# Attention's gate: the sigmoid as ScalarE's exponential, with a sum and a reciprocal on VectorE

## What is computed

```python
def diff_attention(q, k, v, rel_bias, lam, lam_init, subln_w):
    ...
        logits = jnp.einsum('bqhmd,bkhmd->bhmqk', q_blk, k).astype(jnp.float32) * scale + bias
        p = jax.nn.softmax(logits, axis=-1)
        attn = p[:, :, 0] - lam * p[:, :, 1]
        return jnp.einsum('bhqk,bkhd->bqhd', attn.astype(v.dtype), v)
    ...
    o = rmsnorm(o, subln_w) * (1.0 - lam_init)

# in hybrid_layer
    proj = jnp.einsum('bsd,de->bse', h, w_in)      # q, k, v and the gate's input ag among it
    o_a = diff_attention(...)
    o_a = o_a * jax.nn.silu(ag)
```

## Time and profile before

| | |
|---|---|
| runs | 3447.71, 3453.41, 3459.82 us (median 3453.41) |
| profiled execution | 3451.49 us |
| its span, from first to last instruction | 3449.7 us |
| mean granted TensorE clock | 0.981 of full speed |
| TensorE busy | 3276.7 us, 95% |
| VectorE busy | 1852.2 us, 54% |
| ScalarE busy | 1423.0 us, 41% |
| GpSimd busy | 436.3 us, 13% |
| attention, layer 0 | 1957 to 2301 us of the span |
| attention, layer 1 | begins some 750 us later |

### The profile page before, as it was taken

One profiled execution on the slowest core, in us unless ns is written; L12 is line 12 of the kernel. 1 busy time (PEld: TensorE's weight loads), 2 busy tenths in 40 slices (PEclk: granted clock), 3 DMA queues, 4 the chain that ended last, 5 costly groups with the idle time before them and its releaser, 6 DMA issues. The chain is left out here.

```text
span 3449.7 us, 73665 instructions
## 1 busy us (share of the span) xinstructions
PE 3276.7 (95%) x32618; PEld 2033.5 (59%) x32618; DVE 1852.2 (54%) x2557; ACT 1423.0 (41%) x2045; POOL 436.3 (13%) x302
## 2 busy tenths in 40 slices
PE   6999999999899797999999899999999999999999
PEld 3446565644444346999886466657644466657544
DVE  4666767662526524666553566654453366754342
ACT  3554545433655422333333445542322255533321
POOL 3000000020000002334331132300000232200000
PEclk9999999999999998999999999999999999999999
DMA  5111111130355552111112111021021211020211
GB/s 177 37 49 46 39 39 34 43 118 17 98 127 123 123 139 77 68 68 56 58 46 87 55 32 54 7 60 32 17 91 49 68 43 37 1 66 26 65 67 49
DMA packets 308210, 214.84 MB, mean 62 GB/s; under 512 B 125403, under 2 KB 283950, under 8 KB 305326
## 3 DMA queue, kind: packets, MB, share of 16 engines
q1 hardware_dynamic: 307464, 210.18, 20.4%
q10 hardware_dynamic: 458, 0.37, 0.0%
HBM read 172.74 MB, written 41.98 MB: 62 GB/s over the span
## 5 line engine op out<-in xcount | busy, mean ns | idle before, releaser
L142 PE MATMUL psum<-u,w_hi 128*128 128x512 f16 x1856 | 555.5, 381 | 17.3 <-PEq L197 5.4
L142 PE MATMUL psum<-u,w_lo 128*128 128x512 f16 x928 | 353.3, 381 | 0.0
L142 PEld LDWEIGHTS psum<-u,w_hi 128*128 128x128 f16 x1856 | 181.4, 98 | 245.8 <-issue 23.0
L115 DVE SCALAR_TENSOR_TENSOR w_lo<-stage,w_hi 128x1024 f16<-128x1024 f32 x140 | 170.4, 1238 | 217.1 <-ACT w_hi L109 216.5
L174 PE MATMUL psum<-u,w_hi 128*128 128x512 f16 x896 | 271.4, 381 | 0.0
L2650 DVE CUSTOM_DVE_ANT_0 probs_att<-psum,bias_att 128x1024 f32<-128x1024 f32 x128 | 156.8, 1225 | 165.4 <-PE psum L2445 165.0
L1071 PE MATMUL psum<-w_hi,merged 128*128 128x512 f16 x768 | 233.4, 382 | 6.8 <-PEq L3072 4.5
L2423 PE MATMUL psum<-u,w_hi 128*128 128x512 f16 x768 | 232.2, 384 | 6.7 <-PEq L1109 6.7
L1071 PE MATMUL psum<-held_hi_out,merged 128*128 128x512 f16 x768 | 231.2, 379 | 0.0
L97 POOL TENSOR_TENSOR w_hi<-stage,w_scale 128x1024 f16<-128x1024 f32 x36 | 69.1, 1920 | 946.6 <-PE psum L2423 839.3
L190 PE MATMUL psum<-w_hi,u 128*128 128x128 f16 x2048 | 173.2, 219 | 0.0
(11 more groups left out here) (463 smaller groups left out, 6987.6 us busy)
## 6 DMA issues: line engine op xcount, KB each, us to landing
stage<-w_in SPq DMA_DIRECT2D x72, 512.0 KB, 5.0
X<-rwkv_chunks SPq DMA_DIRECT2D x14, 1792.0 KB, 8.1
stage<-ab_w_in SPq DMA_DIRECT2D x48, 512.0 KB, 4.8
stage<-rw_w_in SPq DMA_DIRECT2D x32, 512.0 KB, 4.7
rwkv_chunks<-work_rp SPq DMA_DIRECT2D x26, 512.0 KB, 5.9
stage<-w_out SPq DMA_DIRECT2D x24, 512.0 KB, 4.2
X<-x SPq DMA_DIRECT2D x16, 512.0 KB, 8.5
stage<-ab_w_out SPq DMA_DIRECT2D x16, 512.0 KB, 4.7
```

The lines of the kernel that those rows point to most:

```text
L115: dve.scalar_tensor_tensor(K.w_lo[:, slot, :], K.stage[:, slot, :], W_SCALE, K.w_hi[:, slot, :], ALU.mult, ALU.subtract).then_inc(K.w_full ...
L142: last = pe.matmul(K.psum[:, bank, :], w[:, k, :], u[:, k, cols], start=(k == 0 and n == 0), stop=(k == KT - 1 and n == 2))
```

## The change

ScalarE computes exp(-x) in place of sigmoid(x), and no longer loads the set behind it. VectorE adds 1 and takes the reciprocal, in place on `gate`, and then multiplies as before. Each of the two new instructions is followed by a drain, which lets VectorE finish writing before the next one reads. Nothing else differs; the order of the work is as it was.

```diff
--- before.py
+++ after.py
@@ -2548,10 +2548,8 @@
                     else:
                         if g >= 2:
                             act.wait_ge(part_done, 2 * (g - 1))
-                        act.activation(gate[g % 2][:, cols(half)], bank, ACT.Sigmoid, scale=UNSCALE
+                        act.activation(gate[g % 2][:, cols(half)], bank, ACT.Exp, scale=-UNSCALE
                                        ).then_inc(g_sig, 1)
-                        if g or half:
-                            act.preload_act_table_set("natural_log_exp_and_others")
 
                 def exponentials(s):
                     for m in range(2):
@@ -2637,6 +2635,10 @@
                     elif slot == 3:
                         x = gate[g % 2][:, cols(half)]
                         dve.wait_ge(g_sig, g * 2 + half + 1)
+                        dve.tensor_scalar(x, x, 1.0, None, ALU.add)
+                        dve.drain()
+                        dve.reciprocal(x, x)
+                        dve.drain()
                         dve.scalar_tensor_tensor(x, bank, UNSCALE, x, ALU.mult, ALU.mult).then_inc(taken[half], 1)
 
                 def with_bias(s):
```

## The result

The changed kernel takes 3471.02 us (median of 8 runs, 3462.15 to 3475.42), the kernel before 3448.76 us (median of 8, among them the three shown above). The medians differ by 22 us. The ratio is 1.0059, with a 95% interval of 1.0046 to 1.0073: slower by about 20 us (16 to 25). The forecast was 3467 us, 15.8 us slower.

A forecast was written before the change was run, and what follows sets the result against it. TensorE sets attention's pace, so only late releases count: 9.2 us at heads 1 and 2, 4.8 at head 3, 1.8 at head 0, sum 15.8 us on 3451.49, giving 3467.3 us; range 3457 to 3481.

The forecast's parts named there:

- The table loads at nothing: ScalarE, gates: 28 removed loads of 1.283 us, 35.9 us in all, were costed at no gain.
- The price of a half: VectorE, each of 16 gate halves: sum 0.45, two drains 0.18, reciprocal 3.4, together 4.03 us more.
- The slope of 6.25 ns a column: VectorE's reciprocal: growth from 8 to 12 columns extended to 512, giving 3.35 us; 3.4 us taken.
- Heads 1 and 2: Four gates, both layers: TensorE 2.3 us late at each through late bank releases, 9.2 us in all.
- the first wait: Heads 1 and 2: TensorE waits 0.8 us for the bank released by the first half's product.
- the second wait: Heads 1 and 2: TensorE waits 1.5 us for the second half's release, 2.3 us late in all.
- Head 0: Two gates: first half just in time, bias sums late for TensorE's logits by 0.9 us; 1.8 us in all.
- the rival with GpSimd: Head 0: GpSimd holds the new sum for all three operations, 4.3 us more a layer, 3476 us; chance 0.08.
- Head 3: Last head, two gates: second half's late release delays the next stage 1.9 us in layer 0, 2.9 in layer 1; 4.8 us.
- A reciprocal that is fast at length: VectorE: 512 columns take some 0.7 us, nothing reaches TensorE, 3451.5 us; chance 0.10.
- The loads on the path: ScalarE's table loads delay TensorE, so up to 35.9 us come back, 3431 us at the best; chance 0.04.
- The clock: Heads 1 and 2: granted clock falls behind the new waits, adding 10 to 20 us, 3477 to 3487 us; chance 0.08.

The follow-up runs named there:

- ScalarE's half: Changed kernel without VectorE's sum and reciprocal, exponent scaled down by 1000: exponential for sigmoid, 28 table loads fewer. Ratio to the kernel before 0.9991.
- the last one: Kernel before, sigmoid and table loads kept, with only two order changes at the last head, on ScalarE and VectorE: 3439.28 us, ratio 0.9976.
- the gate of exp, Ln and exp: Changed kernel with ScalarE computing the whole sigmoid as exp, Ln, exp in one table set, no VectorE sum or reciprocal: ratio to before 0.9996.
- the late gate: Changed kernel with the same sums and reciprocals on VectorE behind the bank's release, which ScalarE gives after copying the value: ratio to before 1.004.
- half the columns: Changed kernel with the reciprocal over 256 of each half's 512 columns, exponent scaled down by 1000: ratio to before 1.0021.
- the reciprocal is doubled: Changed kernel with a second reciprocal and drain behind the first, exponent scaled down: ratio to before 1.0256.
- ScalarE's order alone changed: Sigmoid from ScalarE's exp, Ln, exp, with finished values taken ahead of exponentials in steps 24 and 28: ratio to before 0.9986.

## Why the prediction was right

**Point by point.** The table loads at nothing: right, by the experiment on ScalarE's half and by the last one. The price of a half, 4.03 us: right; it is 0.427 + 3.353 + two gaps of 0.08, 3.94 us. The slope of 6.25 ns a column, taken from 4 columns' difference, held up to 512. The reciprocal of 128x512 is not the 4.27 us that eight cycles a column would make of the Trainium skill's repeat count ("VectorE: DVE Perf Modes", "First, the fixed hardware budget"): 6.25 ns are six cycles at its 0.96 GHz.

Heads 1 and 2: 2.3 forecast, 2.48 measured four times. The steps are all there: the first wait (0.8, measured 0.77), the bias sum without its idle time, the small product that swallows the lateness behind GpSimd (1.93 us became 1.11), the second wait (1.5, measured 1.58). The 0.2 us missing come from two small things that I left out: GpSimd's operations, behind which the second half stands, end 0.3 us later (above), against 0.1 us by which a half is cheaper than forecast, and TensorE starts 0.06 us behind the end of the second product. (The prediction's step of "about 9.4 us" is 9.67 us between the two times that it gives; nothing in the sum rests on it.)

Head 0: 0.9 forecast, 0.73 measured. The sum met GpSimd as foreseen. VectorE's and GpSimd's timelines:

```profile
1999.15 1.15 DVE L2638 TENSOR_SCALAR merged<-merged 128x512 f32<-128x512 f32 x1
2000.37 3.35 DVE L2640 RECIPROCAL merged<-merged 128x512 f32<-128x512 f32 x1
```

```profile
1998.12 1.89 POOL L97 TENSOR_TENSOR w_hi<-stage,w_scale 128x1024 f16<-128x1024 f32 x1 [5.66 <-PE psum L2423]
2000.17 1.89 POOL L99 TENSOR_TENSOR stage<-stage,w_scale 128x1024 f32<-128x1024 f32 x1 [0.16 <-issue]
```

The sum issued at 1999.15 ends at 2000.30, 1.15 us and not 0.43: it waited for the operation that ended at 2000.01, and GpSimd's next one began at 2000.17. It got in after one operation, not after three, so the rival with GpSimd is out. That agrees with the exclusive lock by order of arrival of the Trainium skill ("SBUF — State Buffer", "Who interferes with whom").

Head 3 is the term that was mis-sized: 4.8 us forecast for both layers, 6.9 measured up to step 31 and 7.5 up to the last `norm`. TensorE's timeline in layer 0 and the windows to it (the last number but two is the granted clock):

```profile
2242.10 2.04 PE L2473 MATMUL psum<-turned_att,merged 128*128 128x128 f32 x8 [4.49 <-ACT sq_att L2571]
...
2248.18 1.01 PE L174 MATMUL psum<-u,w_hi 128*128 128x512 f16 x2 [1.35 <-issue]
...
2274.62 1.64 PE L2473 MATMUL psum<-turned_att,merged 128*128 128x128 f32 x8 [1.95 <-ACT sq_att L2571]
```

```profile
2241.00:2251.00 10.00, 7.54 (x30) 0.50 0.01 2
...
2275.00:2278.00 3.00, 3.00 (x15) 0.51 0.00 0
```

The wait for the squares grew from 3.39 to 4.49, as forecast (4.7). The piece starts 2.5 us late by the release, where 1.9 were forecast: the second half does not stay where it was. Its sum starts 0.65 us later, 0.3 of it by GpSimd as at heads 1 and 2, the rest by a pause of 0.45 us within the combination for which the profile shows no cause. What I put at nothing is the clock. Before, the granted clock is 0.50 for 6.8 us at this head in layer 0 and for 3.4 us in layer 1. Now it is 0.50 for 10.2 us and, behind the wait for the squares of step 28, for 3.4 us more in layer 0, and for 6.8 us in layer 1. Because of the first stretch the logits of step 28, 7 us behind the piece, are 3.5 us late and not 2.5. The second stretch makes the 0.6 us at step 31 and the 0.7 us behind it: the kernel before has full speed there, although its wait was longer (2.29 us). Of the low stretches TensorE works through 8.9 us before and 15.8 now, by the windows; half of the difference, an estimate of 3.5 us, is the clock's price. The waits of this head grew by 4.2 us.

In layer 1 the number (2.9 forecast, 2.7 measured) is better than the account: the piece starts 3.2 us late there, and 0.5 us of it come back because the clock is full again when it starts (2999.63 to 3000.20, a row of four transposes, takes 0.74 us before and 0.60 now). How long the clock stays low is not settled. Behind the wait of 3.39 us, in the four kernels that have it (the one before, ScalarE's half, the gate of exp, Ln and exp, the late gate), it was 3.4 us six times and 6.8 twice. Behind 4.45 to 4.49 us it was 6.8 us four times and 10.2 twice. The two of 10.2 are in layer 0 of the kernels that wait there a second time, 1.35 us for the gate's product; with half the columns that wait is missing and the stretch is 6.8 us. In layer 1 the second wait of 0.98 us changed nothing. So the longer wait goes with a longer stretch, and the part of the second wait is not shown.

Sum: 15.8 forecast for waits. TensorE's waits in attention grew by 14.8 us, and about 3.5 us of low clock came on top; the lags gained up to the last `norm` are 18.9, with the 0.6 us by which the first logits already stood later (the clock is low for the first 5.5 and 4.5 us of the two attentions, and was for 5.3 and 3.7) 19.5, and the ratio says 20 (16 to 25). That the time forecast, 3467 us, is nearer to the median of 3471 than the difference is to the measured one is luck: the profiled execution from which it starts is 2.7 us above the median of the eight.

**The rivals.** A reciprocal that is fast at length: out, 3.353 us. The loads on the path: out. The clock: not at heads 1 and 2 of this kernel, where it stays at full speed behind the waits of 0.77 and 1.58 us, but some 3.5 us at head 3, and, with products that take 32 us longer, enough for the whole surplus when the reciprocal is doubled. Its mechanism was right and its place wrong. The prediction named a fall of the clock behind the new waits as a sign of being wrong; at head 3 that sign is there in part.

## What to carry to other kernels

Ask of an added instruction not on which engine it lies but what stands behind it in the same queue: here 4 us sat between a wait and the release of a PSUM bank, against a slack of 1.8 us, while 36 us of table loads on a half-idle engine were worth nothing. Count the slack to the next consumer first, and then look at what the added time shifts: the half reciprocal would have cost little by its slack, but with it another instruction met GpSimd's. Price the clock too where TensorE already waits for some us: the stretches at half speed were longer behind 4.5 us of waiting than behind 3.4. A value that the same table set can give (exp, Ln, exp) is the cheaper way to a sigmoid when VectorE holds the release.

## What the runs showed of the hardware

- The reciprocal on VectorE takes 6.25 ns a column from 8 to 512 columns (202 and 227 ns at 8 and 12, 1754 ns at 256, 3353 at 512), about five times the gate's product of the same length (692 ns).
- The length of one wait did not decide by itself whether TensorE's granted clock fell to 0.50, the 1.2 GHz level. In these attentions it stayed full behind waits of 0.77, 1.58, 2.29, 2.63 (the gate's product, with ScalarE's order alone changed) and 3.43 us, and was at 0.50 behind waits of 2.50 (twice), 3.39 (eight times) and 4.20 us (four times). Behind 1.95 us both are seen: full in layer 1 of the changed kernel, 0.50 in layer 0.
- Where the low clock sets in moved too: behind the same wait of 3.39 us, the eight products took 2.05 us in layer 0 of the kernel before and 1.13 in its layer 1, where the clock fell 1.3 us after TensorE had resumed.
- VectorE's low part (128x512), begun while a GpSimd operation ran, took 2.24 us in place of 0.68 (half the columns), and a GpSimd operation begun while the low part ran took 2.18 us in place of 1.89 (the changed kernel).
- Doubling the added work made the loss four times as large: a slack and the clock both bend the line, in the same direction.
